# Three edits to the attention of a streaming encoder on one core: pipeline depth by tile, order of the first key loads, an empty step in the index plan

## What is computed

```python
def dsa_attend(q, qi, wt, q_pos, k, v, ki, topk):
    s = einsum('bqhd,bld->bqhl', qi, ki) * IDX_DIM ** -0.5
    score = einsum('bqhl,bqh->bql', relu(s), wt * IDX_HEADS ** -0.5)
    score = where(adm, score, -inf)                 # chunk-causal
    _, idx = top_k(score, topk)                     # 256 prompt, 132 sample
    logits = einsum('bqhgd,bqjhd->bqhgj', q, k[idx]) * HEAD_DIM ** -0.5
    p = softmax(logits)
    return einsum('bqhgj,bqjhd->bqhgd', p, v[idx])

def reference(...):
    # layer 0: dsa on prompt (1024 frames) and sample (past 512 + 16 new), residual, MLP
    # layer 1: gated linear attention, residual, MLP; final RMSNorm
```

## Time and profile before

| | |
|---|---|
| median of 3 runs | 2818.42 us (2817.14 to 2819.47) |
| the profiled execution | 2823.1 us |
| its span, first to last instruction | 2821.2 us, mean granted TensorE clock 0.993 |
| TensorE busy | 97% |
| VectorE, ScalarE, GpSimd busy | 71%, 46%, 13% |
| attention phase | 321 to 641 us |
| transfers | 279 MB, mean 99 GB/s |

### The profile page before, as it was taken

One profiled execution on the slowest core, in us unless ns is written; L12 is line 12 of the kernel. 1 busy time (PEld: TensorE's weight loads), 2 busy tenths in 40 slices (PEclk: granted clock), 3 DMA queues, 4 the chain that ended last, 5 costly groups with the idle time before them and its releaser, 6 DMA issues. The chain is left out here.

```text
span 2821.2 us, 43795 instructions
## 1 busy us (share of the span) xinstructions
PE 2734.0 (97%) x16007; PEld 2405.3 (85%) x16007; DVE 2010.4 (71%) x3073; ACT 1302.6 (46%) x2140; POOL 368.2 (13%) x389
## 2 busy tenths in 40 slices
PE   8899999999999999999999999999999999999998
PEld 8889877667889988999888988877888999889987
DVE  4389789843597789877975166637269877887787
ACT  3277668882344444544442144434133544445433
POOL 2222011110000000000012155447000000000000
PEclk9999999999999999999999999999999999999999
DMA  4422531234132322223214333347312323222231
GB/s 151 115 55 92 142 81 24 46 90 157 58 121 78 105 81 75 92 81 110 70 54 147 102 111 115 124 138 278 112 67 91 102 73 109 71 85 80 92 103 74
DMA packets 202173, 279.04 MB, mean 99 GB/s; under 512 B 29282, under 2 KB 138786, under 8 KB 202035
## 3 DMA queue, kind: packets, MB, share of 16 engines
q1 hardware_dynamic: 201890, 276.68, 30.7%
q10 hardware_dynamic: 144, 0.52, 0.1%
HBM read 220.13 MB, written 57.03 MB: 98 GB/s over the span
## 5 line engine op out<-in xcount | busy, mean ns | idle before, releaser
L1671 DVE TENSOR_TENSOR h<-mlp_dn_acc,h 128x512 f32<-128x512 f32 x308 | 200.9, 684 | 19.9 <-PE mlp_dn_acc L1522 19.1
L1522 PE MATMUL mlp_dn_acc<-end_w_hi,early 128*128 128x512 f32 x400 | 157.8, 395 | 0.0
L1522 PE MATMUL mlp_dn_acc<-end_w_hi 128*128 128x512 f32 x392 | 155.1, 396 | 2.7 <-DVE end_w_lo L1644 1.4
L1522 PE MATMUL mlp_dn_acc<-end_w_lo,end_w_hi 128*128 128x512 f32 x392 | 155.0, 395 | 0.0
L660 PE MATMUL acc<-mid_w_hi,mid_xT_hi 128*128 128x512 f32 x320 | 130.7, 409 | 2.7 <-DVE mid_xT_lo L246 2.1
L660 PE MATMUL acc<-mid_w_lo,mid_xT_hi 128*128 128x512 f32 x320 | 125.5, 392 | 0.0
L660 PE MATMUL acc<-mid_w_hi,mid_xT_lo 128*128 128x512 f32 x320 | 125.4, 392 | 0.0
L2962 ACT ACTIVATE att_logits<-att_logits,att_neg_max 128x528 f32<-128x528 f32 (+8 forms) x144 | 111.3, 773 | 23.6 <-DVE att_neg_max L3025 23.1
L2934 ACT ACTIVATE att_probs_T<-att_psT 128x512 f32<-128x512 f32 (+3 forms) x224 | 98.6, 479 | 39.7 <-PE att_psT L2835 36.9
L1522 PE MATMUL mlp_dn_acc<-mid_w_hi 128*128 128x512 f32 x294 | 114.4, 389 | 0.0
L1522 PE MATMUL mlp_dn_acc<-mid_w_hi,mid_w_lo 128*128 128x512 f32 x294 | 114.4, 389 | 0.0
(11 more groups left out here) (595 smaller groups left out, 9197.2 us busy)
## 6 DMA issues: line engine op xcount, KB each, us to landing
mlp_pool_w<-x_sums SPq DMA_DIRECT2D x84, 576.0 KB, 3.7
mlp_pool_w<-in_ffn_w_up SPq DMA_DIRECT2D x42, 512.0 KB, 4.7
spare_w<-in_ffn_w_down SPq DMA_DIRECT2D x32, 512.0 KB, 3.8
proj_w_raw<-in_a_w_in SPq DMA_DIRECT2D x8, 1024.0 KB, 6.0
mid_w_raw<-in_ffn_w_down SPq DMA_DIRECT2D x16, 512.0 KB, 4.3
end_w_raw<-in_ffn_w_down SPq DMA_DIRECT2D x16, 512.0 KB, 4.0
x_sums<-mlp_pool_w SPq DMA_DIRECT2D x24, 288.0 KB, 2.1
spare_w<-in_b_w_in SPq DMA_DIRECT2D x6, 1024.0 KB, 7.0
```

What stands on the lines that cost most here:

```text
L1522: mm = pe.matmul(dst, lhs(c, f), rhs(a, f), start=(n == 0 and not onto), stop=(n == 2 * len(TERMS) - 1), skip_group_check=onto)
L1671: dve.tensor_tensor(dst, acc, dst, ALU.add).then_inc(added, 1)
```

## The change

1. In the planner an empty list is put behind the first entry of `steps`, so that one unit has no sample step behind it.
2. In attention the depth between `logits` and `turn` becomes `lag(n)`: 3 for the heads of the sample and of tiles 3, 0 and 2, and 2 for the others. `values`, `oT_copy`, `turn_back` and `finish` of a quad move with it. In the sample's steps `stream_values` comes one head later (n - 4) and ahead of `turn`; `finish` of the sample's groups comes one step later.
3. In tile 3 the copies of the odd heads' turned probabilities go from ScalarE to VectorE. The copies stay in order, by waits on `turned_out`.
4. SyncE issues the keys of stream 2 first, and the prompt's keys as two transfers of 512 KB, the second behind keys 3. GpSimd waits for each half.

```diff
-        steps = [[("s_new", 0, 0), ("s_turn", 0, 0)]]
+        steps = [[("s_new", 0, 0), ("s_turn", 0, 0)], []]
...
-    VALUES_AT = {quad_at(q) + 6 + 2 * half: (q, half) for q in range(NQ) for half in range(2)}
-    OUT_AT, BACK_AT, FINISH_AT = ({quad_at(q) + later: q for q in range(NQ)} for later in (9, 10, 11))
+    DEEP = (SAMPLE, 3, 0, 2)
+    lag = lambda n: 3 if tile_at(n) in DEEP else 2
+    TURN_AT = {}
+    for n in range(N):
+        TURN_AT.setdefault(n + lag(n), []).append(n)
+    VALUES_AT = {quad_at(q) + lag(quad_at(q)) + 4 + 2 * half: (q, half) for q in range(NQ) for half in range(2)}
+    OUT_AT, BACK_AT, FINISH_AT = ({quad_at(q) + lag(quad_at(q)) + later: q for q in range(NQ)} for later in (7, 8, 9))
+    on_dve = lambda n: tile_at(n) == 3 and n % 2 == 1
+    DVE_FROM = start_of[3]
...
-        if n >= 2:
-            nb = -(-length(n - 2) // (4 * P))
-            bank_of[n - 2] = list(range(banks, banks + nb))
+        for m in TURN_AT.get(n, ()):
+            nb = -(-length(m) // (4 * P))
+            bank_of[m] = list(range(banks, banks + nb))
             banks += nb
...
+                def load_prompt_keys(tiles):
+                    sp.dma_start(kin[:, tiles, :, :].rearrange("p t v d -> p t (v d)"),
+                                 k_out.rearrange("(t p) c -> p t c", p=P)[:, tiles, :]).then_inc(k_loaded[tiles.start * 2 // NT_P], 16)
+
+                load_keys(2)
                 load_values(0)
                 sp.dma_start(nv[:, :, :], v_new.rearrange("(b t) c -> t b c", t=DEC_T)).then_inc(new_v_in, 16)
-                sp.dma_start(kin[:, :, :, :].rearrange("p t v d -> p t (v d)"), k_out.rearrange("(t p) c -> p t c", p=P))\
-                    .then_inc(k_loaded, 16)
-                load_keys(2)
+                load_prompt_keys(slice(0, NT_P // 2))
                 load_values(1)
                 load_keys(3)
+                load_prompt_keys(slice(NT_P // 2, NT_P))
...
-                pool.wait_ge(k_loaded, 16)
                 for r in range(NT_P):
+                    pool.wait_ge(k_loaded[r * 2 // NT_P], 16)
...
                         logits(n)
-                    if 2 <= n < N + 2:
-                        turn(n - 2)
-                    if 3 <= n < HEADS + 3:
-                        stream_values(n - 3)
+                    if 4 <= n < HEADS + 4:
+                        stream_values(n - 4)
+                    for m in TURN_AT.get(n, ()):
+                        turn(m)
...
                 def turn_out(n):
                     for x, i in enumerate(bank_of[n]):
+                        if n > DVE_FROM:
+                            act.wait_ge(turned_out, i)
                         act.wait_ge(turned, i + 1)
...
-                    if 2 <= n < N + 2:
-                        turn_out(n - 2)
+                    for m in TURN_AT.get(n, ()):
+                        if not on_dve(m):
+                            turn_out(m)
...
+                def turn_out(n):
+                    for x, i in enumerate(bank_of[n]):
+                        dve.wait_ge(turned_out, i)
+                        dve.wait_ge(turned, i + 1)
+                        dve.wait_ge(values_done, (n - HEADS) // GH4 - 1)
+                        out, turned_bank = turned_parts(n, x, i)
+                        dve.tensor_copy(out, turned_bank).then_inc(turned_out, 1)
...
-                    if GH4 <= n < HEADS + GH4 and n % GH4 == GH4 - 1:
-                        finish(n // GH4 - 1)
+                    for m in TURN_AT.get(n, ()):
+                        if on_dve(m):
+                            turn_out(m)
+                    if GH4 < n <= HEADS + GH4 and n % GH4 == 0:
+                        finish(n // GH4 - 2)
```

More of the change, by code:

```diff
@@ L2585, in attention_phase @@
     key_bank, prep_bank, bank_of, banks = {}, {}, {}, 1
-    for n in range(-1, N + 2):
+    for n in range(-1, N + 3):
         if n + 1 < N and tile_at(n + 1) == SAMPLE:
@@ L2655, in attention_phase @@
         pv = b.ps("pv", [P, 2, 512])
-        k_loaded, v_loaded = b.sem("k_loaded"), b.sem("v_loaded")
+        k_loaded, v_loaded = [b.sem("k_loaded0"), b.sem("k_loaded1")], b.sem("v_loaded")
         q_loaded = [b.sem("q_loaded0"), b.sem("q_loaded1")]
@@ L2667, in attention_phase, with turned_parts @@
         o_stored = [last_stored, b.sem("o_stored1")]
+        def turned_parts(n, x, i):
+            c0, c1 = 4 * x * P, min(4 * (x + 1) * P, length(n))
+            rows = P if (c1 - c0) % P == 0 else c1 - c0
+            cols = max(c1 - c0, P)
+            return probs_T[0:rows, probs_slot(n), c0:c0 + cols], psT[0:rows, i % 2, 0:cols]
         with b.program() as block:
@@ L2930, in turn_out @@
                             act.wait_ge(values_done, (n - HEADS) // GH4 - 1)
-                        c0, c1 = 4 * x * P, min(4 * (x + 1) * P, length(n))
-                        rows = P if (c1 - c0) % P == 0 else c1 - c0
-                        cols = max(c1 - c0, P)
-                        act.activation(probs_T[0:rows, probs_slot(n), c0:c0 + cols], psT[0:rows, i % 2, 0:cols], ACT.Copy)\
-                            .then_inc(turned_out, 1)
+                        out, turned_bank = turned_parts(n, x, i)
+                        act.activation(out, turned_bank, ACT.Copy).then_inc(turned_out, 1)
                 def oT_copy(q):
@@ L2941, in oT_copy @@
                     act.activation(oT[:, q % 2, :], pv[:, q % 2, 0:2 * P], ACT.Copy).then_inc(oT_out, 1)
-                for n in range(-1, N + 6):
+                for n in range(-1, N + 7):
                     if n + 1 in key_bank:
@@ L3005, in _ @@
                                     q_new[HD:P, pair, :, :].rearrange("p g (b t) -> p g b t", t=DEC_T)).then_inc(qs_done, 1)
-                for n in range(N + 8):
+                for n in range(N + 9):
                     if n < N:
```

1 line of the change is left out of this document (added).

## The result

| | before | after |
|---|---|---|
| median of 8 runs | 2819.34 us (2817.14 to 2822.09) | 2827.07 us (2824.01 to 2830.40) |
| span of the profiled execution | 2821.2 us | 2828.4 us |
| its mean granted clock | 0.993 | 0.994 |

The ratio is 1.0026, 95% interval 1.0017 to 1.0035: the changed kernel is slower by 0.26%, outside the predicted range and on the side that had 0.16. The predicted holes came; what was missed is a sum of smaller terms, the largest of them depth 3 in the sample, with its seam to tile 7.

The account below looks back on a forecast made before the run. It took TensorE, busy 97% of the span, as the bound, with VectorE full from 390 to 551 us. Terms 0 - 2.5 - 3.6 + 9.0 - 0.5 - 1.0 - 0.5 - 0.2 = +0.7 gave 2819.1 us, range 2809 to 2825.

Parts of the forecast that it names:

- Part 4: Seam from sample to tile 7, depth 3 to 2: one value product less before logits 19; -0.5 us, ends -1.5 and +1.
- the prediction's own first paragraph: Whole kernel: time is won only where TensorE has a hole, runs at low clock or waits for a full engine.
- Part 3b: Sample's steps: next keys wait for ScalarE's copy to free a psT bank, 0.82 us in 11 steps; +9.0 us.
- The rival that they don't come: Sample's steps: the holes do not appear and the rest of the sum stands, -8.3, 2810.1 us; chance 0.20.
- Part 3a: Sample's step 8: later `finish` removes the 1.9 us wait for `k_lo` and 1.7 of low clock behind it; -3.6 us.
- Part 2: Sample's loads: wait of 3.2 us for keys of stream 2 becomes 1.6; -2.5 us, ends -3.3 and 0.
- Part 1: Planner's list, TensorE's holes near 131.8 us: the empty step costs 0, ends -3.4 and +0.5 us.
- Part 5: Tiles 3, 0 and 2: -1.0 for copies on VectorE, -0.5 for tile 0's entry, -0.2 in tiles 0 and 2.
- The clock rival: Sample's stage: holes in 11 steps bring the clock down to 0.83; +10.1, 2828.5 us; chance 0.15.
- the likeliest case: Whole kernel: the forecast itself, alone 2814 to 2824 us, chance 0.50.

Follow-up runs that it names:

- deep_free: keys_finish_deep with ScalarE's copies of tile 7's first three heads no longer waiting for the sample's last value product: ratio 0.9991.
- keys_finish: Kernel before with the new order of the loads and the later `finish`, depth 2 everywhere: ratio 0.9985, 2815.9 us.
- keys_finish_deep: keys_finish with the sample at depth 3 and its value products behind the transpose: ratio 0.9999, 2819.6 us.
- values_behind: Changed kernel with the sample's value products behind the step's transpose of probabilities, except the last: ratio 1.0002, 2818.9 us.
- only_empty: Kernel before with only the empty step of the index plan added: ratio 1.0006.
- only_tiles: Kernel before with only depth 3 in tiles 3, 0 and 2 and half of tile 3's copies on VectorE: ratio 1.0002.
- only_finish: Kernel before with only the `finish` of each quad of the sample one step later: ratio 0.9995.
- only_keys: Kernel before with only the new order of the loads, keys of stream 2 first and prompt keys in halves: ratio 0.9990.

## Why the prediction was wrong, step by step

| part | forecast | by the ratios | what it was |
|---|---|---|---|
| 1, empty step | 0 | +1.4 | 0.84 us more wait at attention's start, which comes 1.2 us later on average |
| 2, loads | -2.5 | -2.8 | right in size; by the trace only 1.0 of it where it was forecast |
| 3a, `finish` | -3.6 | -1.4 | wait at step 8 from 1.9 to 0.8 alone and 0.4 with the loads; over-sized |
| 3b, holes | +9.0 | +6.9 | ten, 0.3 to 0.85 each |
| 4, depth 3 and its seam | -0.5 | +3.8 | one more head on TensorE in a full stage, and a wait; some 2 us stay open |
| 5, last tiles | -1.7 | 0.0 | not seen in the times; some 1.5 shorter by the traces |
| sum | +0.7 | +7.9 | measured +7.3 and +6.5 |

**Part 4 is the step that failed.** The prediction said that TensorE has one value product less in its way to logits 19, which is a gain of 1.5 us for one step, and that ScalarE's copy of head 16 waits "as before" for a product that lies a step later, which it priced at nothing. (With the 0.6 us of waiting its own terms give -0.9, of which it took -0.5.) What it left out is that depth only moves work. At the sample's start one step passes without a transpose and one without values, and at the seam the stage of tile 7 gets that head on top of its own: 322 matmuls became 337. In a uniform kernel the two cancel. Here they don't, because VectorE is full in tile 7 (its 48.9 us of 49.8): every microsecond that it stands there is lost for good, by the prediction's own first paragraph, while at the start TensorE stands in other waits, and the stage before the seam became only 0.65 us shorter (386.63 - 322.64 against 385.93 - 322.59). 2.52 - 0.65 = 1.9 us by the traces, deep_free showing how the 2.5 divide into 0.9 and 1.6. The ratios of the three pairs say 2.8 to 4.5. What they have beyond 1.9 us does not lie in the sample or tile 7. The profiled executions of keys_finish and keys_finish_deep lasted just the median of their kernels, and their spans differ by 4.0 us (2813.8 and 2817.8). TensorE's first transpose behind attention, in each:

```profile
637.82 3.31 PE L262 MATMUL out_psT<-ident,spare_x 128*128 128x128 f32 x16 [1.42 <-PEq L2683]
638.83 1.94 PE L262 MATMUL out_psT<-ident,spare_x 128*128 128x128 f32 x16 [1.42 <-PEq L2683]
```

So +1.0 us stands up to there (1.9 to tile 6, 0.8 back in the last tiles) and +3.0 behind it, in phases that neither edit touches. Over all eighteen traces these phases took 2179.2 us on average in the nine kernels with the sample at depth 3, and 2177.6 in the other nine, with 2175.9 to 2181.0 as the ends. Whether the depth does this, and by what, stays open.

**Part 3b was right in mechanism, place and sign**, and a little large: eleven holes of 0.82 were forecast. The first trace of the change holds ten (5.8 us), the second eleven (6.4 us), but the eleventh, at step 4, is in values_behind too, so ten are the order's. They cost 0.73 to 0.85 us a step, and at step 8, where the hole lies partly in place of the wait for `k_lo`, 0.3 (5.06 for 4.75), which makes 7.2 us. The rival that they don't come is refuted.

**Part 3a was over-sized.** Its 1.9 us of idle time held nearly (0.4 was left in values_behind, at depth 3). The 1.7 us for the clock did not appear as time by the ratios, and they were not this part's alone: behind step 8, between 350 and 370 us, 1.7 us were lost to the low clock in before, only_empty and only_tiles, but none in only_finish, and none in only_keys either, where the wait is still 1.5 us. Against the gain stand the 0.6 us by which tile 7's stage grew; the step before it shrank by 0.4. By the traces `finish` moved gives 2.0 and 2.3 us. The part had assumed depth 3 for the wait to vanish; depth 2 with the later `finish` and the loads in time leaves 0.4, so depth was not needed.

**Part 2 held** at -2.8 for -2.5, in part by luck. Of the 2.9 us by which only_keys is shorter to tile 6, only 1.0 lies where the gain was forecast, between the maskings of steps 2 and 4 (9.6 us for 10.6); the other 1.9 lie between those of steps 7 and 9 (10.1 for 12.0), where the wait for `k_lo` is 0.4 shorter and no low clock follows it. One input was off as well. GpSimd's copy was to start at 329.6 as before, 8.5 us behind attention's first transpose; it starts 9.7 behind it (334.05 - 324.36 in after). This is no price of the halves: with the new order it starts 9.6 to 9.8 us behind in all fourteen traces, with the old one 8.3, 8.5, 9.9 and 10.1 behind (only_tiles, before, only_empty, only_finish), so before's single trace had one of the early ones. TensorE came to it later as well: the wait is 1.2 us in only_keys, and the forecast 1.6 in values_behind and in the second trace of the change. As to the rule of the Trainium skill (DMA: Bandwidth & Descriptors, Queues, rings and completion order) that descriptors are taken in ring order but need not finish in it: no run shows the keys of stream 2 overtaken. In after TensorE waits for no DMA in the sample's stage.

**Part 1** has its 0.84 us where the prediction never looked. It followed the steps moved among TensorE's holes at 131 us and did not ask what the other end of the planner's list does. Why VectorE ends later there, presumably since the sample's steps end one unit later in the list, no run isolates.

**Part 5** counted 1.2 us (-0.2 in tiles 0 and 2 and -1.0 in tile 3) for small stops, and 0.5 for a shorter hole before tile 0. The first trace of the change has both entries at a clock of 1.00; the second, of the same kernel, lost 1.7 us at the entry of tile 3. At the entry of tile 0 the clock stayed up in all eleven traces with Part 5, which the prediction had as its better case (-2.2 in place of -0.5). So the part's -1.7 may be right by the traces; the times, 0.0 with some 2 us to either side, neither confirm nor refute it. The prediction's statement that the wait into tile 3 moves into `values` was right:

```profile
586.84 0.65 PE L2883 MATMUL att_pv<-att_probs_T,att_v_in 128*64 128x256 f32 x4 [3.24 <-ACT att_probs_T L2952]
```

answers the 3.08 of rows 11.

**The clock rival** (it falls in the sample's stage because of the holes, 2828.5 us) came within 1.5 us of the measured time and is wrong in its reason: in 344 to 394 us of after, with ten holes, the granted clock is 1.00, and none of the other four traces with the holes lost clock from 350 to 394. The Trainium skill (TensorE: Matmul & The Clock Gate, A second HAM failure mode: psum-queue depth-cycling) tells of one kernel with brief idling between groups whose clock swung; holes of 0.58 us in steps of 4.5 to 5 did not do it here.

The range failed with the sum: Part 4 had +1 as its upper end where +3.8 came, the whole of 3a was taken at the end with the clock, and the upper bound of the likeliest case, 2824, allowed 5 us for six terms of which, by the ratios, four came out above their forecast.

## What to carry to other kernels

Raising or lowering the depth of a software pipeline at a stage's edge moves one item's work across that edge, so cost it in the stage that receives it; if an engine is full there, the move is paid and not won back. When an operation changes places with another on an engine, ask which transfer through a ring of two banks the old neighbour covered, since that cover is lost in every step. Judge such changes by a part-by-part set of timed kernels: terms of 1 to 3 us are the size by which two traces of the same kernel differ. Then compare each stage's length over all their traces at once: that showed Part 5's 1.5 us, which three timed pairs left open, and that the 1.2 us between before and after in a transfer's landing are no price of the new order.

## What the runs showed of the hardware

Low clock came mostly in amounts of 1.7, 3.4 or 5.1 us of lost full-speed time and at different places in different executions of one program. The change, unaltered, had a granted clock of 0.66 from 324 to 334 us once and of 0.85 once, its spans being 2828.4 and 2823.4 us. One stretch hardly ever changed: behind the index steps' hole near 131 us, 3.4 us or more were lost in each of the eighteen traces. Holes of 0.58 us, ten in a row, brought no low clock from 350 to 394 us in any of five traces. Behind a wait of 1.9 us at step 8, 1.7 us were lost in three traces of three; behind one of 1.5 (only_keys) and one of 0.8 (only_finish) none. And the same 1664 KB, in two orders, let GpSimd start 9.6 to 9.8 us behind attention's first transpose in fourteen traces of the new order, and 8.3 to 10.1 behind in four of the old: one trace is too few for such a difference.
